# The output projection's two seams: the last window job scaled by pairs on GpSimd, tile 0 normed inside attention, three weight blocks rounded there, two gate banks computed ahead

## What is computed

```python
def merge_heads(o_fox, o_nsa, g, w_out):
    o = jnp.concatenate([rmsnorm(o_fox, g[:FOX_W]), rmsnorm(o_nsa, g[FOX_W:])], axis=-1)
    return o @ w_out
...
    o = gates[:, :, 0][..., None] * o_c + gates[:, :, 1][..., None] * o_s + gates[:, :, 2][..., None] * o_w
...
    xp = xp + merge_heads(o_fox, o_nsa, out_norm_g[l], w_out[l])
...
    gu = rmsnorm(x, g_norm) @ w_gu
    g, u = gu[..., :D_FF], gu[..., D_FF:]
```

## Time and profile before

| | |
|---|---|
| median of 3 runs | 1965.08 us (1964.33 to 1965.45) |
| the profiled execution | 1964.52 us, of which the span from first to last instruction 1962.8 |
| busy, share of the span | PE 92%, PEld 81%, DVE 50%, ACT 38%, GpSimd 26% |
| granted TensorE clock, mean | 0.978 of full speed |

### The profile page before, as it was taken

The page is one execution under the profiler, slowest core; times in us unless marked ns, Lnnn a source line. Parts: engine busy times, 40 slices in busy tenths (PEclk is TensorE's granted clock), DMA queues, the critical chain, the costliest instruction groups (busy, mean ns, idle before and its releaser), DMA issues. The chain is left out here.

```text
span 1962.8 us, 31183 instructions
## 1 busy us (share of the span) xinstructions
PE 1808.4 (92%) x11465; PEld 1594.4 (81%) x11465; DVE 990.1 (50%) x1909; ACT 740.3 (38%) x1477; POOL 504.7 (26%) x604
## 2 busy tenths in 40 slices
PE   4999999998878789999997998999999999999996
PEld 4898777998644678888886887999999999976784
DVE  4233421333343777777777542333333333375997
ACT  3234411211322377777777332111112111243453
POOL 5020032421444532222212101211112221133523
PEclk9799999999999899999998998999999999999999
DMA  8544343356967973333312121111111111164543
GB/s 185 80 107 156 119 154 117 114 165 214 351 233 266 205 206 71 66 65 65 93 38 79 66 88 42 52 53 43 43 43 43 43 53 53 46 229 146 202 136 142
DMA packets 169903, 229.30 MB, mean 117 GB/s; under 512 B 45018, under 2 KB 113477, under 8 KB 169665
## 3 DMA queue, kind: packets, MB, share of 16 engines
q1 hardware_dynamic: 143298, 152.77, 26.1%
q0 software_dynamic: 24400, 72.81, 13.1%
q10 hardware_dynamic: 2080, 2.10, 0.4%
HBM read 192.65 MB, written 40.24 MB: 119 GB/s over the span
## 5 line engine op out<-in xcount | busy, mean ns | idle before, releaser
L121 PE MATMUL gate_acc<-o_T_hi,w_gate_split_hi 128*128 128x352 f32 x528 | 171.5, 325 | 2.3 <-ACTq L2817 2.3
L121 PE MATMUL up_acc<-o_T_hi,w_up_split_hi 128*128 128x352 f32 x528 | 170.6, 323 | 0.7 <-DVEq L2881 0.7
L122 PE MATMUL gate_acc<-o_T_lo,w_gate_split_hi 128*128 128x352 f32 x528 | 170.3, 323 | 0.0
L123 PE MATMUL gate_acc<-o_T_hi,w_gate_split_lo 128*128 128x352 f32 x528 | 170.2, 322 | 0.0
L122 PE MATMUL up_acc<-o_T_lo,w_up_split_hi 128*128 128x352 f32 x528 | 169.2, 321 | 0.0
L123 PE MATMUL up_acc<-o_T_hi,w_up_split_lo 128*128 128x352 f32 x528 | 169.1, 320 | 0.0
L2305 ACT ACTIVATE pa_scores<-pa_scores,pa_neg_max 128x128 f32<-128x128 f32 (+1 forms) x192 | 143.5, 747 | 16.6 <-DVE pa_neg_max L2345 13.2
L2393 DVE TENSOR_TENSOR pa_probs_T_lo<-pa_t,pa_probs_T_hi 128x512 fp32r<-128x512 f32 (+2 forms) x240 | 124.0, 533 | 29.3 <-ACT pa_probs_T_hi L2320 27.1
L2939 POOL TENSOR_TENSOR w_gate_split_lo<-w_gate,w_gate_split_hi 128x1024 fp32r<-128x1024 f32 x21 | 50.4, 2400 | 341.5 <-ACT w_gate_split_hi L2827 341.5
L2320 ACT ACTIVATE pa_probs_T_hi<-pa_t 128x512 fp32r<-128x512 f32 (+2 forms) x240 | 110.8, 476 | 67.8 <-PE pa_t L2244 64.8
L2244 PE MATMUL pa_t<-ident,pa_scores 128*128 128x128 f32 x688 | 115.7, 275 | 20.6 <-DVE pa_probs_T_lo L2393 19.8
(11 more groups left out here) (456 smaller groups left out, 4828.5 us busy)
## 6 DMA issues: line engine op xcount, KB each, us to landing
w_down_raw<-in_w_down SPq DMA_DIRECT2D x59, 512.0 KB, 4.5
fox_k_pages<-in_cache_fox_kv SPq DMA_DIRECT2D x64, 256.0 KB, 5.7
w_rows<-in_cache_fox_kv POOLq DMA_DIRECT2D x48, 256.0 KB, 4.8
w_gate<-in_w_gu SPq DMA_DIRECT2D x22, 512.0 KB, 3.9
w_up<-in_w_gu SPq DMA_DIRECT2D x22, 512.0 KB, 3.9
w_rows<-in_w_in SPq DMA_DIRECT2D x5, 2048.0 KB, 8.5
sel_pages<-in_cache_nsa_kv POOLq DMA_DIRECT2D x64, 128.0 KB, 5.5
pa_k_fox<-scratch_kf_d POOLq DMA_DIRECT2D x32, 256.0 KB, 6.8
```

Source lines behind the costliest of these rows:

```text
L121: pe.matmul(out, a[0][at], b[0][bt], start=start, stop=False)
L122: pe.matmul(out, a[0][at], b[1][bt], start=False, stop=False)
L123: return pe.matmul(out, a[1][at], b[0][bt], start=False, stop=stop)
```

## The change

The arithmetic stays; places and owners of steps move.

1. *The last job by pairs.* DVE forms reciprocal and factors for each of the last job's four pairs as soon as the pair is summed (`last_pair`). GpSimd multiplies the first three pairs and adds them to `o_prompt`; DVE does so for the fourth.
2. *Tile 0 in attention's tail.* When the first pair has been added, tile 0 is complete. ACT loads the root table and squares tile 0 before its copy of the last pair, DVE forms the mean (`first_mean`) before the last pair's sum, ACT takes the root, DVE norms tile 0 (`first_scale`) before the last pair's factors, and PE turns tile 0 into two PSUM banks (`c.tp`) that outlive the phase. Copy and rest of the turned tile (`copy_first`, `rest_first`) are the head of the next phase, in halves.
3. *Weights.* ACT rounds blocks 0 to 2 at the end of attention, and DVE takes the rest of block 0 there. In the projection GpSimd has blocks 1, 3, 5 and DVE 2, 4, 6, 7; DVE norms tile 1 between 4 and 6, ACT squares and takes the root of tile 1 between the rounding of 4 and 5.
4. *PE's order.* `product(0)` comes first and `turn_o(1)` stands before its block 5.
5. *Gate columns ahead.* The gate columns of block 0 were 72 matmuls at the head of the gate phase. Now 24 of them (`first_gate(0)`) stand between `turn_x(7)` and `turn_x(8)`, 24 (`first_gate(1)`) behind `turn_x(8)`, both into `c.tp`, and 24 remain in the gate phase.

```diff
@@ prompt_attention
-        PT = [ph.ps(f"pa_t{i}", [P, 4 * P]) for i in range(2)]
+        PT = [c.tp[:, i, :] for i in range(2)]
@@ gpsimd, behind the last turn
+            for n in range(PJ - 1):
...
+                pool.wait_ge(s_pc, n + 1)
+                pool.tensor_tensor(rows, rows, coef, ALU.mult).then_inc(s_pm, 1)
+                pool.wait_ge(s_pm, n + 1)
+                pool.tensor_tensor(dst, dst, rows, ALU.add).then_inc(s_on, 1)
@@ tensor, at the end
+            pe.wait_ge(s_cd, NCK)
+            for n in range(KD):
+                if n % 4 == 0:
+                    pe.wait_ge(s_f5, n // 4 + 1)
+                pe.transpose(PT[n // 4][:, n % 4 * P:(n % 4 + 1) * P], c.o[:, 0, n * P:(n + 1) * P], c.ident[:, :])
@@ scalar
-            act.activation(rt[:, 0:1], c.one[:, :], ACT.Sqrt)
+                if s == NU + 3:
+                    act.activation(rt[:, 0:1], c.one[:, :], ACT.Sqrt)
+                    act.wait_ge(s_on, 1)
+                    for w_ in range(2):
+                        act.activation(sc[0][:, w_ * 512:(w_ + 1) * 512], c.o[:, 0, w_ * 512:(w_ + 1) * 512], ACT.Square,
+                                       accum_out=first[0][:, w_:w_ + 1]).then_inc(s_f1, 1)
+
+            act.wait_ge(s_f2, 1)
+            act.activation(first[2][:, :], first[1][:, :], ACT.Sqrt).then_inc(s_f3, 1)
+            act.wait_ge(s_o, (NH - 1) * NJ * PJ + 5 * PJ + 1)
+            for n in range(3):
+                act.wait_ge(c.s_wo[n], 16)
+                act.activation(c.wo[0][:, n, :], c.op_raw[:, n, :], ACT.Copy).then_inc(s_wr0, 1)
@@ vector
+                if p == NPR - 1:
+                    first_scale()
+                if i == NH - 1 and j == NJ - 1:
+                    last_pair(p, s, t, j)
...
+                dve.wait_ge(s_wr0, 1)
+                dve.tensor_tensor(c.wo[1][:, 0, :], c.op_raw[:, 0, :], c.wo[0][:, 0, :], ALU.subtract)
@@ output_and_norm
+        W_POOL, W_DVE = (1, 3, 5), (2, 4, 6, 7)
...
+                    if t == 0 and k % 4 == 0:
+                        pe.wait_ge(s_l1, k // 4 + 1)
+                    if t == 0 and k == 5:
+                        turn_o(1)
...
+            def first_gate(n):
+                bank = c.tp[:, n, 0:CH]
+                pe.wait_ge(gate.s_lo[0], 1)
+                pe.wait_ge(s_l1, NR + 1)
+                pe.wait_ge(s_l2, math.ceil((n + 1) * CH / P))
+                for k in range(KD):
+                    split_products(pe, bank, gate.ws[0], oT, np.s_[:, k, :], np.s_[:, k, n * CH:(n + 1) * CH], k == 0, k == KD - 1)
+
+            product(0)
+            for step in range(2, NR + 2):
...
+                if step == NR:
+                    first_gate(0)
+            first_gate(1)
@@ output_and_norm, scalar
+            for k in range(2):
+                copy_first(k)
+            for k in range(3, 5):
+                round_w(k)
+            squares_o(1)
+            root_o(1)
+            for k in range(5, KD):
                 round_w(k)
@@ output_and_norm, vector
+            for k in range(2):
+                rest_first(k)
+            rest_w(2)
+            rest_w(4)
             scale_o(1)
-            rest_o(0)
...
+            for k in (6, 7):
+                rest_w(k)
@@ gate_up
-            products(0, 0, G_, s_g, s_gc)
+            products(0, 0, gate_bank, s_g, s_gc, 2)
             tables()
```

More of the change, by code:

```diff
@@ L2087, in prompt_attention @@
         s_ch = ph.sem("pa_chain")
+        s_on = ph.sem("last_pairs_added")
+        s_f1, s_f2, s_f3, s_f4, s_f5 = (ph.sem(f"o_first_{n}_done") for n in ("squares", "mean", "root", "inverse", "normed"))
+        s_wr0 = ph.sem("w_out_first_rounded")
+        s_pc, s_pm = ph.sem("last_pair_coef"), ph.sem("last_pair_scaled")
         block = ph.block()
@@ new lines, in first_mean, with first_scale @@
+            def first_mean():
+                dve.wait_ge(s_f1, 2)
+                dve.tensor_scalar(first[1][:, :], first[0][:, :], 2.0 / D, EPS, ALU.mult, ALU.add).then_inc(s_f2, 1)
+            def first_scale():
+                dve.wait_ge(s_f3, 1)
+                dve.reciprocal(first[3][:, :], first[2][:, :]).then_inc(s_f4, 1)
+                dve.wait_ge(s_f4, 1)
+                dve.wait_ge(c.s_g1, 16)
+                for w_ in range(2):
+                    at = np.s_[w_ * D // 2:(w_ + 1) * D // 2]
+                    dve.scalar_tensor_tensor(out=c.o[:, 0, at], in0=c.o[:, 0, at], scalar=first[3][:, w_:w_ + 1], in1=c.op_g1[:, at],
+                                             op0=ALU.mult, op1=ALU.mult).then_inc(s_f5, 1)
@@ L2510, in root_o, with copy_first @@
             def root_o(t):
-                act.wait_ge(s_ms1, t + 1)
+                act.wait_ge(s_ms1, t)
                 act.activation(st1[2][0:ROWS[t], t, :], st1[1][0:ROWS[t], t, :], ACT.Sqrt).then_inc(s_rt1, 1)
+            def copy_first(k):
+                act.activation(oT[0][:, 4 * k:4 * k + 4, 0:P], turned(tp1, 0)[:, 4 * k:4 * k + 4, :], ACT.Copy).then_inc(s_c1, 1)
             def copy_o(t):
-                act.wait_ge(s_t1, t + 1)
+                act.wait_ge(s_t1, t)
                 act.activation(tile(0, t), turned(tp1, t), ACT.Copy).then_inc(s_c1, 1)
@@ L2622, in _ @@
         def _(pool):
-            for k in range(0, KD, 2):
-                pool.wait_ge(s_wh, k + 1)
+            for k in W_POOL:
+                if k > 2:
+                    pool.wait_ge(s_wh, k - 2)
                 pool.tensor_tensor(wo[1][:, k, :], raw[:, k, :], wo[0][:, k, :], ALU.subtract).then_inc(s_wp, 1)
@@ L3433, in build @@
                 compressed_attention(c, pa)
+                c.tp = late.ps("turned_rows", [P, 2, 512])
                 prompt_attention(c, pa)
```

134 lines of the change are left out of this document (77 added, 57 removed).

## The result

The changed kernel took 1953.70 us (median of 8 runs, 1950.60 to 1957.53), the kernel before beside it 1964.11 us (8 runs, 1959.79 to 1966.99): ratio 0.9946, 95% interval 0.9934 to 0.9958, faster by 10.4 us. The forecast was 1955.2.

A forecast was written before the change was run, and what follows sets the result against it. Inside the output projection only PE's work was taken to count, with PE's waits at two seams to shorten. Gains of 2.8 and 7.1 made 9.9 us: 1965.1 - 9.9 = 1955.2 us, range 1952.6 to 1960.

The forecast's parts named there:

- two seams: Attention to output projection, judged by the start of `turn_o(2)`, gain 2.8 us; around `turn_x(8)` and gate products, gain 7.1.
- Attention's tail: End of attention: ACT's last copy 0.85 us late, DVE done at 1067.1, projection starting at 1068.4, 2.7 us later.
- pair factors: Last job's reciprocals and factors by pairs on DVE: 0.45 us in sum, bounds 0 and 1.1.
- Barrier: Between attention and the projection: takes 1.33 us, as before.
- First product: Projection's head: PE starts at 1069.8 instead of 1075.25, with 2.5 us for a start at the low clock.
- DVE against PE: First seam: both engines' chains let `turn_o(2)` start at 1084.5, together a little later, 1085.0; gain 2.8 us, bounds -1.4 and 4.9.
- contended rest: First seam: a DVE weight rest takes 3.1 us beside GpSimd's, 1.22 alone.
- Second seam: From `turn_x(8)` to the tables: 10.4 us instead of 17.52, gain 7.1, bounds 4.2 and 7.4.
- The tables: Behind the gate products: loads have 3.9 us of cover instead of 14; no wait taken, bound 2.9 us.
- Weight rests do bind: Rival, chance 0.14: GpSimd and DVE collide throughout, first seam gives -1.4 to 0.5 us, time near 1959.
- the low clock at the second seam: Rival, chance 0.13: tables late or clock low, second seam gives only 4.2 to 5 us, time near 1957.7.
- a product stuck at the low clock: Rival, slower, chance 0.04: PE stays at the low clock, `product(0)` ends at 1092.4; near 1973 with the next product wholly low.

The follow-up runs named there:

- gap_filled: Changed kernel with first_gate(0) computed in the gap but thrown away and all 72 gate matmuls run again behind the barrier; one run, 16.00 us from `turn_x(8)` to the tables.
- weights_late: Changed kernel with the early rounding of blocks 0 to 2 (ACT) and block 0's rest (DVE) back in the projection; 1955.64 us, ratio 0.9959.
- tile1_first: Changed kernel with the squares and norm of tile 1 moved ahead of weight block 4 on ACT and DVE; 1954.08 us, ratio 0.9950.

## Why the prediction was right

The forecast of the two seams was 2.8 + 7.1; the trace shows 2.94 + 7.43. The median came out 1.5 us below the forecast: 0.5 by the gains, and 1.0 because the kernel before, in 8 runs instead of 3, stands at 1964.1, not 1965.1. By steps:

- *Attention's tail.* Forecast 0.45 us on PE for the pair factors. Behind the first pair PE waited for ACT, not DVE. The norm of tile 0, the last factors and block 0's rest ended at 1067.43, that is R + 14.01; forecast 1067.1, R + 14.3. ACT's last copy started at 1062.54, R + 9.12, before at 1061.31, R + 8.50: 0.62 late, forecast 0.85. GpSimd's pair steps (0.40 and 0.46) were as short as forecast, but they were not off the path: the prediction let nobody wait for the second and third pair, and the phase's end does, since GpSimd's DRAIN ended 5.3 us behind the last of them, at R + 14.0, level with DVE. Before, a DRAIN as far behind the last addition was over at 1059.4, 5 us ahead of DVE's end. That DVE's forecast end held for the phase is luck.
- *Barrier.* Forecast 1.33 as before, measured 1067.43 to 1069.13 = 1.7. This took back what the tail had gained on its forecast: the projection starts at R + 15.7, forecast 1068.4 or R + 15.6.
- *First product.* Forecast 1069.8 or R + 17.0, measured R + 17.08, with seven slow products from PE's 4.41 us of idle time: cost 7 x (0.427 - 0.233) = 1.4 us, forecast 2.5.
- *DVE against PE.* Both chains were put at 1084.5 (R + 31.7) and the seam half a microsecond behind. PE's was ready at R + 31.2 and DVE's at R + 32.0, so DVE's norm released `turn_o(2)`, one of the two outcomes named. **The term that was mis-sized is the contended rest.** The prediction priced it at 3.1 us, the mean of three on either engine, as two engines slowing each other. The runs show each held by the other's whole instruction: DVE's rests stood still for 0.4, 0.9 and 1.9 us in place of a common rate, and the first of them, block 2, took 1.62. That the sum came out within 0.3 us is partly luck. Block 2 was priced 1.5 us too long, and the sum had no wait of DVE in front of block 4, where it waited 1.23 for ACT, and ACT 1.56 for the block's load; block 4 ended at R + 22.5, as forecast.
- The Trainium skill (SBUF — State Buffer, "SBUF: two separate sides") describes just this lock, for a whole instruction of either engine. The runs agree, with the 2.33 us of DVE's 128x2 operation and the 3.38 us of GpSimd's second rest. By that rule the prediction had `turn_o(2)` near 1085.6, R + 32.8; measured R + 32.07.
- *Second seam.* Forecast 10.4 from `turn_x(8)` to the tables, measured 10.09: the barrier took 1.44, not 1.6, and `turn_x(8)`, at full clock, less. The tables cost nothing, though their loads were issued only from 1197.65 on: 0.18 us behind the last gate product PE turned the first.
- *Rivals.* Weight rests do bind the first seam, but at the forecast gain, not near zero. Neither the tables, nor the low clock at the second seam, nor a product stuck at the low clock came; `gap_filled` shows that the low clock was a live danger there, and five of the nine traces with both banks ahead met it right behind the tables, where the prediction had everything keep its distances.

## What to carry to other kernels

Price a seam by what is late last behind it, not by the first instruction that moves: here the early norm of tile 0 was worth nothing without the early weights. Before work is given to GpSimd, look in the trace whether DVE's instructions beside it are stretched; three rests on GpSimd cost DVE as much standstill as it would have spent on them. Where a phase ends at a barrier, look at each engine's DRAIN and not only at its last operation: GpSimd's ended 5.3 us behind its last addition. And where runs spread by several us, measure an edit of a few us by positions from an event just ahead of it.

## What the runs showed of the hardware that was not expected

- A 128x2 operation of DVE can take 2.33 us instead of 0.16 when a GpSimd operation on 128x1024 operands runs.
- GpSimd's DRAIN at the end of attention ended 5.3 us behind its last addition, before, after and in `weights_late`. What it waits for was not tried.
- From the last engine's end to the first operation behind the barrier it took 1.33 us before and 1.7 after. What makes the difference was not tried.
- The granted clock fell after 2.34 us of idle PE in one execution and not after 2.37 us in another, behind the same work. Runs of slow products differed in length too: 7 to 13 at the first product of the kernels that have the new first seam, 0 to 18 at the gate products. So the price of a low clock read from one trace is one draw: 1.4 us at the first product in both traces of the changed kernel, some 2.5 in `tile1_first`.
- R itself, over a thousand us behind the start, stood anywhere from 1045.7 to 1055.1 us; the two traces of the changed kernel differ by 5.8 us in span (1952.5 and 1946.7), 4.5 of them in R.
